# Last tile of both networks in buffers of its own, and another order of the final norm

## What is computed

```python
def conv_glu_ffn(h, w_in, conv_w, conv_b, w_out):
    ...
    gate = c[..., :FFN_DIM]
    val = c[..., FFN_DIM:]
    return (jax.nn.silu(gate) * val) @ w_out
...
        x = x + conv_glu_ffn(h, ffn_w_in[l], ffn_conv_w[l], ffn_conv_b[l], ffn_w_out[l])
...
    return rmsnorm(x, final_norm_g)
```

## Time and profile before

| what | us |
|---|---|
| three runs | 647.74, 646.80, 646.96 (median 646.96) |
| span of the profiled execution, first to last instruction | 645.1 |
| TensorE busy | 629.7 |
| VectorE busy | 528.7 |
| ScalarE busy | 417.3 |
| GpSimd busy | 36.3 |

### The profile page before, as it was taken

The page is one execution under the profiler, slowest core; times in us unless marked ns, Lnnn a source line. Parts: engine busy times, 40 slices in busy tenths (PEclk is TensorE's granted clock), DMA queues, the critical chain, the costliest instruction groups (busy, mean ns, idle before and its releaser), DMA issues.

```text
span 645.1 us, 10742 instructions
## 1 busy us (share of the span) xinstructions
PE 629.7 (98%) x3614; PEld 527.9 (82%) x3614; DVE 528.7 (82%) x953; ACT 417.3 (65%) x817; POOL 36.3 (6%) x90
## 2 busy tenths in 40 slices
PE   9999999999999999999999999979999999999995
PEld 8998766678888888888887888768988888888894
DVE  4588688857999888889888646877899898888887
ACT  6554577847766666666677464884866666666666
POOL 1100021200000000000012000150000000000000
PEclk9999999999999999999999999999999999999998
DMA  8677040034455555555525544603455555555521
GB/s 326 250 255 276 2 197 2 1 131 163 164 201 192 196 196 196 196 196 195 173 89 194 197 156 177 250 40 127 168 196 197 196 196 194 189 179 189 189 71 66
DMA packets 21456, 109.11 MB, mean 169 GB/s; under 512 B 2608, under 2 KB 2992, under 8 KB 12464
## 3 DMA queue, kind: packets, MB, share of 16 engines
q1 hardware_dynamic: 21136, 108.48, 47.1%
q10 hardware_dynamic: 288, 0.22, 0.1%
HBM read 107.64 MB, written 1.05 MB: 168 GB/s over the span
## 4 chain that ended last, share of the span: by engine, by line
PE 87%; DVE 8%; ACT 3%; issue 1%; POOL 1%; DVEq 0%; ACTq 0%; POOLq 0%
PE psU L674 21%; PE psA L463 13%; PE psA L464 13%; PE psA L465 13%; PE psU L679 10%; PE psU L900 2%; PE psA L860 1%; PE psU L885 1%; PE psU L474 1%; DVE arena L2107 1%; ACT arena L1500 1%; DVE arena L1818 1%; PE psA L791 1%; PE psU L654 1%; PE psU L653 1%
## 5 line engine op out<-in xcount | busy, mean ns | idle before, releaser
L674 PE MATMUL psU<-hA,win_hi 128*128 128x512 f32 x608 | 190.8, 395 | 0.0
L679 PEld LDWEIGHTS psU<-hA,win_lo 128*128 128x128 f32 x608 | 114.2, 188 | 26.6
L679 PE MATMUL psU<-hA,win_lo 128*128 128x256 f32 x608 | 119.4, 278 | 0.0
L1792 DVE TENSOR_TENSOR win_lo<-stage,win_hi 128x1024 fp32r<-128x1024 f32 x86 | 104.8, 1221 | 0.0
L674 PEld LDWEIGHTS psU<-hA,win_hi 128*128 128x128 f32 x608 | 95.3, 189 | 2.8
L1290 ACT ACTIVATE win_hi<-stage 128x1024 fp32r<-128x1024 f32 x89 | 93.3, 1050 | 5.5 <-PE psA L465 5.5
L1818 DVE SCALAR_TENSOR_TENSOR arena<-arena,prm 128x255 f32<-128x255 f32 (+1 forms) x168 | 77.2, 480 | 3.7 <-ACT arena L1302 0.7
L1700 DVE TENSOR_TENSOR win_lo<-stage,win_hi 128x1024 fp32r<-128x1024 f32 (+3 forms) x50 | 55.8, 1153 | 15.7 <-ACT win_hi L1218 15.5
L463 PE MATMUL psA<-wout_hi,act_hi 128*128 128x512 f32 x168 | 65.9, 392 | 0.3
L464 PE MATMUL psA<-wout_lo,act_hi 128*128 128x512 f32 x168 | 65.6, 390 | 0.0
L465 PE MATMUL psA<-wout_hi,act_lo 128*128 128x512 f32 x168 | 65.4, 389 | 0.0
(11 more groups left out here) (315 smaller groups left out, 1130.8 us busy)
## 6 DMA issues: line engine op xcount, KB each, us to landing
stage<-in_w_ffn_in SPq DMA_DIRECT2D x44, 1024.0 KB, 4.8
stage_out<-in_w_ffn_out SPq DMA_DIRECT2D x44, 516.0 KB, 5.0
stage<-in_w_kv SPq DMA_DIRECT2D x8, 1024.0 KB, 4.9
stage<-in_w_dq SPq DMA_DIRECT2D x4, 1024.0 KB, 4.9
stage<-in_w_dout SPq DMA_DIRECT2D x4, 1024.0 KB, 4.8
stage<-in_w_group SPq DMA_DIRECT2D x3, 1024.0 KB, 4.9
stage<-in_w_nsa_out SPq DMA_DIRECT2D x3, 1024.0 KB, 4.8
stage<-in_w_phi SPq DMA_DIRECT2D x2, 1024.0 KB, 6.0
```

The lines of the kernel that those rows point to most:

```text
L674: mm(o, win_hi[:, slot, cs], hA[:, k, :, :].rearrange("p a q -> p (a q)"), start=k == 0, stop=False)
L679: last = mm(o[:, 0:S], win_lo[:, slot, cs], hA_hi[:, k2, :], start=False, stop=k2 == KT - 1)
L1792: last = dve.tensor_tensor(win_lo[:, win, cs], stage[:, slot, cs], win_hi[:, win, cs].bitcast(F32), sub)
```

## The change

The last tile's output weights get buffers of their own, `last_w_hi` and `last_w_lo`, in memory of `hB`, which the networks do not use. ScalarE copies the whole high part at the start of `last_steps` instead of in two halves further on; GpSimd subtracts the whole low part, 128x1024, in both layers, instead of VectorE in two halves. In layer 1 TensorE's order becomes: three banks of tile NJ - 2, the stacked products of these three banks, then the fourth bank of tile NJ - 2 and its stacked products (`down_ends`).

In the final norm GpSimd multiplies three quarters by the gain and scales 384 columns of t = 0; VectorE makes the squares of (1,1) with their sum (`tensor_tensor_reduce`), and runs the steps of both Newton iterations mixed; the stores are of 640, 384, 512 and 512 columns. The names of the new slices are `OUT0_ACT` (columns 0 to 639) and `OUT0_POOL` (640 to 1023).

```diff
         final_g = tokA_flat[:, 0:D]
+        last_w_hi, last_w_lo = (w[:, 0:D // S, :].rearrange("p k q -> p (k q)") for w in (hB_hi, hB_lo))
         wo0_hi, wo0_lo = (w[:, :, :].rearrange("p b c -> p (b c)") for w in (wout_hi, wout_lo))
...
             load_ffn(1, C_F1)
-            for i, cs in enumerate(OUT_PIECES):
-                sp.wait_ge(sem["out0_ready"], i + 1)
-                sp.dma_start(a_out[0][:, cs], x[:, 0, cs]).then_inc(sem["stored"], 16)
+            sp.wait_ge(sem["out0_ready"], 1)
+            sp.dma_start(a_out[0][:, OUT0_ACT], x[:, 0, OUT0_ACT]).then_inc(sem["stored"], 16)
+            sp.wait_ge(sem["x_gain"], 1)
+            sp.dma_start(a_out[0][:, OUT0_POOL], x[:, 0, OUT0_POOL]).then_inc(sem["stored"], 16)
             sp.wait_ge(sem["out1_ready"], 1)
-            sp.dma_start(a_out[1][:, OUT_DVE], x[:, 1, OUT_DVE]).then_inc(sem["stored"], 16)
-            sp.wait_ge(sem["stored"], 16 * (len(OUT_PIECES) + 1))
+            sp.dma_start(a_out[1][:, HALVES[1]], x[:, 1, HALVES[1]]).then_inc(sem["stored"], 16)
+            sp.wait_ge(sem["stored"], 16 * 3)
             sp.wait_ge(sem["stored1"], 16)
...
                     cs = slice(n * 512, (n + 1) * 512)
-                    mm(psA[:, 2 * n + t, :], act_hi[:, 1, t * P:(t + 1) * P], wout_hi[:, 1, cs], start=False, stop=False)
-                    return mm(psA[:, 2 * n + t, :], act_hi[:, 1, t * P:(t + 1) * P], wout_lo[:, 1, cs], start=False, stop=True)
+                    mm(psA[:, 2 * n + t, :], act_hi[:, 1, t * P:(t + 1) * P], last_w_hi[:, cs], start=False, stop=False)
+                    return mm(psA[:, 2 * n + t, :], act_hi[:, 1, t * P:(t + 1) * P], last_w_lo[:, cs], start=False, stop=True)
...
                     for i in range(2 * TT):
-                        t, n = (i % 2, i // 2) if layer == 0 else (i // 2, i % 2)
-                        if i == (2 if layer == 0 else 1):
-                            pe_.wait_ge(sem["out_lo"], f0 + NJ)
-                        last = stacked_bank(t, n)
+                        last = stacked_bank(i % 2, i // 2)
                         if i < 3:
                             last.then_inc(sem["y_ready"], 1)
-                        if i == 2 and layer == 0:
+                        if i == 2:
...
+                def down_ends():
+
+                    pe_.wait_ge(sem["a_lo"], f0 + NJ - 1)
+                    pe_.wait_ge(sem["out_lo"], f0 + NJ - 1)
+                    for t, n in ((0, 0), (0, 1), (1, 0)):
+                        down_bank(0, t, n, False, False)
+                    pe_.wait_ge(sem["a_lo"], f0 + NJ)
+                    pe_.wait_ge(sem["last_lo"], layer + 1)
+                    for t, n in ((0, 0), (0, 1), (1, 0)):
+                        stacked_bank(t, n).then_inc(sem["y_ready"], 1)
+                    down_bank(0, 1, 1, False, False).then_inc(sem["out_used"], 1)
+                    stacked_bank(1, 1).then_inc(sem["out_used"], 1)
...
                 down(NJ - 3, 1, False)
-                down(NJ - 2, 0, False)
-                down_last()
+                if layer:
+                    down_ends()
+                else:
+                    down(NJ - 2, 0, False)
+                    down_last()
...
                 pool.tensor_scalar(pr_, pr_, rec[:, u, 0:1], gates[:, t, h0, 1:2], ALU.mult, ALU.mult).then_inc(sem["pool_scaled"], 1)
+            def last_weights_lo(layer):
+
+                pool.wait_ge(sem["out_hi"], (layer + 1) * NJ)
+                pool.tensor_tensor(last_w_lo, stage_out[:, 1, 0:D], last_w_hi.bitcast(F32), ALU.subtract).then_inc(sem["last_lo"], 1)
+
+            last_weights_lo(0)
             pool.wait_ge(sem["in_hi"], 2 * C_KV + 2)
...
+            last_weights_lo(1)
             pool.wait_ge(sem["final_in"], 16)
             pool.wait_ge(sem["x_new"], 2 * TT * X_NEW[4] + 1)
-            pool.tensor_tensor(xs[:, 0, 0:D // 2], x[:, 0, 0:D // 2], final_g[:, 0:D // 2], ALU.mult).then_inc(sem["x_gain0"], 1)
+            for i, (t, h) in enumerate(((0, 0), (0, 1), (1, 0))):
+                if i:
+                    pool.wait_ge(sem["x_new"], 2 * TT * X_NEW[4] + i + 1)
+                pool.tensor_tensor(xs[:, t, HALVES[h]], x[:, t, HALVES[h]], final_g[:, HALVES[h]], ALU.mult).then_inc(sem["x_gain0"], 1)
+            pool.wait_ge(sem["x_gain0"], 2)
+            pool.wait_ge(sem["rstd_t"], TT * ROOTS[4] + 1)
+            pool.tensor_scalar(x[:, 0, OUT0_POOL], xs[:, 0, OUT0_POOL], rstd[:, 0:1], None, ALU.mult).then_inc(sem["x_gain"], 1)
...
                     j = NJ - 2
+                    act.wait_ge(stage_out_full[1], 16 * (f0 + NJ) // 2)
+                    act.activation(last_w_hi, stage_out[:, 1, 0:D], ACT.Copy).then_inc(sem["out_hi"], 1)
                     act.wait_ge(sem["conv_params"], j + (f0 + 1))
...
                     act.activation(silu[0:LAST, 1, :], conv[0:LAST, 1, 0, :], ACT.Silu).then_inc(sem["silu"], 1)
-                    act.wait_ge(stage_out_full[1], 16 * (f0 + NJ) // 2)
+                    act.wait_ge(sem["prod"], f0 + NJ)
                     act.wait_ge(sem["out_used"], f0 + NJ - 2)
-                    act.activation(wout_hi[:, 1, HALVES[0]], stage_out[:, 1, HALVES[0]], ACT.Copy).then_inc(sem["last_hi"], 1)
-                    act.wait_ge(sem["prod"], f0 + NJ)
                     act.activation(act_hi[0:LAST, 1, :], prod[0:LAST, 1, :], ACT.Copy).then_inc(sem["a_hi"], 1)
-                    act.activation(wout_hi[:, 1, HALVES[1]], stage_out[:, 1, HALVES[1]], ACT.Copy).then_inc(sem["out_hi"], 1)
                     if layer == 0:
...
             act.activation(warm, eps, ACT.Sqrt)
-            for t in range(TT):
-                for h in range(2):
-                    square_half(4, t, h)
-                root_of(4, t)
-            act.wait_ge(sem["x_gain0"], 1)
+            square_half(4, 0, 0)
+            square_half(4, 0, 1)
+            root_of(4, 0)
+            square_half(4, 1, 0)
+            act.wait_ge(sem["last_square"], 1)
+            act.wait_ge(sem["mean0"], TT * ROOTS[4] + 2)
+            act.activation(root[:, 1:2], ssqh[:, 3:4], ACT.Sqrt, bias=mean0[:, 1:2], scale=1.0 / D).then_inc(sem["root"], 1)
+            act.wait_ge(sem["x_gain0"], 2)
             act.wait_ge(sem["rstd_t"], TT * ROOTS[4] + 1)
-            for i, cs in enumerate(OUT_PIECES):
-                if i == 1:
-                    act.wait_ge(sem["x_gain"], 1)
-                act.activation(x[:, 0, cs], xs[:, 0, cs], ACT.Copy, scale=rstd[:, 0:1]).then_inc(sem["out0_ready"], 1)
-            act.wait_ge(sem["x_gain1"], 1)
+            act.activation(x[:, 0, OUT0_ACT], xs[:, 0, OUT0_ACT], ACT.Copy, scale=rstd[:, 0:1]).then_inc(sem["out0_ready"], 1)
+            act.wait_ge(sem["x_gain0"], 3)
             act.wait_ge(sem["rstd_t"], TT * ROOTS[4] + 2)
-            act.activation(x[:, 1, OUT_ACT], xs[:, 1, OUT_ACT], ACT.Copy, scale=rstd[:, 1:2]).then_inc(sem["out1b_ready"], 1)
+            act.activation(x[:, 1, HALVES[0]], xs[:, 1, HALVES[0]], ACT.Copy, scale=rstd[:, 1:2]).then_inc(sem["out1b_ready"], 1)
             act.wait_ge(sem["out1b_ready"], 1)
-            act.dma_start(a_out[1][:, OUT_ACT], x[:, 1, OUT_ACT]).then_inc(sem["stored1"], 16)
+            act.dma_start(a_out[1][:, HALVES[0]], x[:, 1, HALVES[0]]).then_inc(sem["stored1"], 16)
...
-                def last_lo(h):
-
-                    cs = slice(h * D // 2, (h + 1) * D // 2)
-                    return dve.tensor_tensor(wout_lo[:, 1, cs], stage_out[:, 1, cs], wout_hi[:, 1, cs].bitcast(F32), sub)
-
                 def last_steps():
...
                     dve.tensor_tensor(prod[0:LAST, 1, :], silu[0:LAST, 1, :], conv[0:LAST, 1, 1, :], ALU.mult).then_inc(sem["prod"], 1)
-                    dve.wait_ge(sem["last_hi"], layer + 1)
-                    last_lo(0).then_inc(sem["last_lo"], 1)
                     dve.wait_ge(sem["a_hi"], f0 + NJ)
                     dve.tensor_tensor(act_hi[LAST:P, 1, :], prod[0:LAST, 1, :], act_hi[0:LAST, 1, :].bitcast(F32), sub).then_inc(sem["a_lo"], 1)
-                    dve.wait_ge(sem["out_hi"], f0 + NJ)
-                    last_lo(1).then_inc(sem["out_lo"], 1)
+                    dve.wait_ge(sem["last_lo"], layer + 1)
+                    dve.sem_inc(sem["out_lo"], 1)
...
             add_last(1, 1)
-            rstd_of_root(4, 0)
+            dve.wait_ge(sem["x_new"], 2 * TT * X_NEW[4] + 4)
+            dve.tensor_tensor_reduce(squares[:, 1, HALVES[1]], x[:, 1, HALVES[1]], x[:, 1, HALVES[1]], 1.0, 0.0, ALU.mult, ALU.add,
+                                     ssqh[:, 3:4]).then_inc(sem["last_square"], 1)
             first_mean(4, 1)
-            dve.wait_ge(sem["x_new"], 2 * TT * X_NEW[4] + 2)
-            dve.tensor_tensor(xs[:, 0, D // 2:D], x[:, 0, D // 2:D], final_g[:, D // 2:D], ALU.mult).then_inc(sem["x_gain"], 1)
-            dve.wait_ge(sem["x_new"], 2 * TT * X_NEW[4] + 4)
-            dve.tensor_tensor(xs[:, 1, OUT_ACT], x[:, 1, OUT_ACT], final_g[:, OUT_ACT], ALU.mult).then_inc(sem["x_gain1"], 1)
```

(76 more changed lines are left out.)

## The result

The changed kernel takes 650.19 us (median; 649.7 to 650.65), the kernel before 647.35 on the same chip: a ratio of 1.0039, 95% interval 1.0027 to 1.0051, or 2.84 us more. The forecast was 649.7, from a before of 646.96, so +2.7.

What follows compares the result with a forecast made beforehand. TensorE, busy 98% of the span, bounds the kernel; the tail is paced by when output can begin to leave. The end's +2.5 and layer 0's +0.2 make 646.96 + 2.7 = 649.7 us; range 646.5 to 650.9.

Steps and rivals of the forecast that it cites:

- Layer 1's taps: Layer 1's network: VectorE's first tap waits for GpSimd's subtraction, ending near 629.45 instead of 628.76; taken as 0.75 us late.
- the stacked activations: Layer 1: 0.75 late, less 0.31 gained by removing VectorE's low half; ready at 635.36 instead of 634.92, net +0.44.
- if the small copy of parameters ahead of it waits too: Layer 1, case at the copy ahead of VectorE's first tap: the tap is then up to 0.9 us late.
- The first addition: Layer 1's end: TensorE starts the stacked products at 635.41 instead of 635.24; first sum ready 0.17 later, at 636.13.
- Layer 0: Layer 0's network end: three splits come 0.22 later and the stall at 339.83 grows; +0.2, bounds -0.31 to +0.35.
- Squares with a sum: Final norm: VectorE's 128x512 squares wait for GpSimd's second product; near 1.3 us instead of 0.7.
- First 128x1 step: Final norm: the first Newton step queues behind GpSimd's third product, its result at 641.45; a step of 1.0 to 1.2 us.
- small steps slip through: Rival: VectorE's large operations wait, its 128x1 steps do not; +1.5 and 0.2, so 648.6; chance 0.17.
- nothing waits: Rival: GpSimd's subtraction does not hold the taps; sum -0.2, so 646.8, at best -1.2; chance 0.22.
- GpSimd keeps its turn: Rival, final norm: GpSimd's three products run to 641.0 without VectorE's squares between them; result 650.1; chance 0.06.
- First store: Final norm: first store issued at 643.2 instead of 640.43, about 2.8 us later.
- GpSimd's scaling of 384 columns: Final norm: taken as 0.70 to 1.05 us, ending by 643.3; VectorE's last product may wait for it.

Runs made afterwards that it cites:

- e3: Changed kernel with three GpSimd fills of 128x1024 in place of its subtraction; 648.98 us against 647.38 for the kernel before, ratio 1.0025.
- e5: Changed kernel with the old final norm, GpSimd subtracting half the columns, VectorE the others behind the last activations; 646.84 us against 647.38 before, ratio 0.999.
- e7: As e6, but all twelve products of the tile ahead come before the stacked ones in layer 1; 647.17 us against 647.5 before, ratio 0.9998.
- e6: As e5, but VectorE subtracts its half in two quarters, the first ahead of the activations' low part; 646.53 us against 647.5 before, ratio 0.9988.
- e9: Network ends of e6 with the changed final norm, GpSimd's second and third gain products replaced by fills; 647.27 us against 647.51 before, ratio 0.9995.
- e4: Changed kernel, but GpSimd's third gain product waits for the first 128 rows' factor; 649.77 us against 647.5 for the kernel before, ratio 1.0033.
- e8: Changed kernel with a fill of 128x512 in place of GpSimd's third gain product; 649.25 us against 647.5 for the kernel before, ratio 1.0027.

## Why the prediction was right, step by step

- **Layer 1's taps** were to be 0.75 late and are 0.77; the stacked activations +0.44, measured +0.42 (VectorE's part from 635.54 with 0.42, so 8.25 after the fixed point; before 634.50 and 0.42, so 7.83). The place was named wrongly: of "the first tap near 628.3 stretched to about 1.2 us" the runs showed nothing. It was the copy of 128x8 that stretched (1.36), which the forecast had only as a case ("if the small copy of parameters ahead of it waits too"), and e3 shows that fills hold this copy as well, which the forecast's reason, two inputs read, does not cover. That the size came out all the same is in part luck: the copy ended with GpSimd's subtraction, where the forecast had the tap wait for the same end.
- **The first addition** was to come 0.17 later and came 0.27 later. The term that failed is the distance from TensorE's first stacked product to the addition, taken from the kernel before as 0.72 (635.24 to 635.96): here it is 0.84 (636.01 to 636.85). The first product after the pause takes 0.50 instead of 0.39, and the second starts 0.34 behind it, where the forecast counts 0.227 from product to product. The last addition (+0.36, from 637.84 to 638.2) came +0.39.
- **Layer 0**: +0.2, measured +0.25. The lower bound of -0.31 was wrong: e3 and e5 to e7, with no delay by GpSimd or next to none, move the stall's end by only 0.07 to 0.08. The trace of e6 shows what holds it then: ScalarE is through with its three splits at 336.19 and stands idle 0.32 for TensorE's transposes (the line at 336.51), where before it went straight on from the splits. The transposes follow the stacked products and their additions, and in layer 0 these keep their place behind the twelve products (first addition 8.80 after the fixed point in both kernels). In the changed kernel those additions and the splits are both late, by 0.27 and 0.24, so that the size of 0.22 does not show which of the two sets the 0.25.
- **Squares with a sum**: "near 1.3", measured 1.19; alone 0.69 and 0.08 (e9), where the forecast took 0.7.
- **First 128x1 step**: 1.0 to 1.2, measured 1.14, and shown by e4 and e8 to be the third product's doing. That decides against "small steps slip through" (648.6) and "nothing waits" (646.8). "GpSimd keeps its turn" falls too: the squares came between the second and the third product.
- **First store**: the forecast has it +2.77 (643.2 against 640.43), apart from layer 0's 0.2; measured 2.57. The time from the last addition to the first store is, by the table, 2.61 before, 4.79 in the changed kernel, 3.86 in e8 (no third product) and 3.37 in e9 (no second one either, and e6's ends). So of the 2.57 some 0.39 come from the ends, 0.93 go with the third product, 0.49 with the second, and 0.76 stay with the order. Squares, first step, factor and store each came within 0.21 of the forecast, counted from the fixed point. The stores gave back 0.19 where the forecast has 0.27, so that its miss of 0.2 shrinks to 0.12 in the span. The 2.8 us of data and the 0.9 behind them stood; the 2.72 that the forecast adds up with stands in no row.
- **GpSimd's scaling of 384 columns**: 0.70 to 1.05 was taken, 1.25 measured; its bound was too low. It cost nothing, since it runs beside the stores' own wait. The last product of VectorE "may wait" for it: it did not (0.75), and the step ahead of it lost 0.3.

## What to carry to other kernels

Before giving GpSimd work, list every VectorE instruction that will overlap it, small ones included: a copy of 128x8 and a step of 128x1 each lost a whole microsecond here, and on a chain of small steps that is where it hurts. Size the piece so that it ends before VectorE's next copy or two-input step (half the columns did, but for 0.1 at the copy), rather than move it to another time, where it met the next step. And ask of a removed wait what was hiding it: 0.27 us of TensorE's waiting was worth nothing until the order of the products changed as well.

## What the runs showed of the hardware

- GpSimd's pure writes hold a VectorE copy from SBUF to SBUF (0.66 for 0.16) but not two-input operations (four taps in 1.92 beside a fill).
- GpSimd's scaling with one input (128x384, 1.25 us) holds VectorE only for about 0.3 at its start: the 128x1 step took 0.47 for 0.16, and the 128x512 product behind it 0.75 while the scaling was still running. Where the product came first, in e4, it took 1.06. The Trainium skill (SBUF — State Buffer, section SBUF: two separate sides) says of a VectorE instruction with two SBUF inputs and a GpSimd one that reads SBUF that whichever starts first gets the shared pair of ports for the whole instruction and the other is blocked fully. By that the step would have been held to the scaling's end, and these rows show otherwise. Why was not tried.
